# Router logits built from unnormalized tiles inside the output projection, shift and token factor applied by rows, and four picked steps in layer 0

## The reference, cut to what matters

```python
def rms_norm(x, g):
    y = x * lax.rsqrt(jnp.mean(x * x, axis=-1, keepdims=True) + NORM_EPS)
    return y * g
def modulate(h, shift, scale):
    return h * (1 + scale) + shift
...
x = x + gt1 * branch_merge(zx, o_attn_x, lp)          # ends in merged @ w_out: the "out" units
hx2 = modulate(rms_norm(x, g_norm2[l]), sh2, sc2)     # norm2
...
s = jax.nn.sigmoid(t @ w_router)                      # t: the rows of hx2 (and hc2)
sel = s + b_router                                    # best group of four, then top 2 in it
for e in range(N_EXPERTS):
    y = (jax.nn.silu(t @ w_gate[e]) * (t @ w_up[e])) @ w_down[e]
    out = out + combine[:, e:e + 1] * y
```

## Time and profile before

| | |
|---|---|
| median of 3 runs | 1436.21 us (1433.32 to 1440.65) |
| profiled execution, its own time | 1435.62 us |
| its span, first to last instruction | 1433.8 us |
| instructions | 19845 |
| busy: PE, DVE, ACT, POOL | 1242.4 us (87%), 630.7 us (44%), 365.8 us (26%), 117.0 us (8%) |
| DMA | 381.52 MB, mean 266 GB/s |
| mean granted clock | 0.949 |

### The profile page before, as it was taken

One profiled execution on the slowest core, in us unless ns is written; L12 is line 12 of the kernel. 1 busy time (PEld: TensorE's weight loads), 2 busy tenths in 40 slices (PEclk: granted clock), 3 DMA queues, 4 the chain that ended last, 5 costly groups with the idle time before them and its releaser, 6 DMA issues.

```text
span 1433.8 us, 19845 instructions
## 1 busy us (share of the span) xinstructions
PE 1242.4 (87%) x8092; PEld 783.1 (55%) x8092; DVE 630.7 (44%) x1124; ACT 365.8 (26%) x589; POOL 117.0 (8%) x107
## 2 busy tenths in 40 slices
PE   3699897899999884999998984887999977998986
PEld 1577576787787431333343334776789832443443
DVE  2627448685546350221131116485886661221222
ACT  2631125334242410100100014532544430000000
POOL 0000000000003020000000002003960200000000
PEclk9899999999999997999999997999999988999998
DMA  9747994222223549698899984785334469999996
GB/s 380 279 190 312 365 394 164 88 91 87 88 88 120 226 185 334 225 395 309 346 334 396 408 347 178 286 324 205 118 123 172 169 273 369 398 388 399 400 418 273
DMA packets 59486, 381.52 MB, mean 266 GB/s; under 512 B 8800, under 2 KB 11300, under 8 KB 19908
## 3 DMA queue, kind: packets, MB, share of 16 engines
q1 hardware_dynamic: 45584, 345.00, 61.4%
q10 hardware_dynamic: 10292, 20.44, 4.5%
q0 software_dynamic: 3520, 14.81, 2.8%
HBM read 362.66 MB, written 44.83 MB: 284 GB/s over the span
## 4 chain that ended last, share of the span: by engine, by line
PE 44%; issue 26%; DMA 13%; DVE 8%; ACT 4%; POOL 3%; SPq 1%; ACTq 0%; POOLq 0%; DVEq 0%
PE bank L1928 9%; PE bank L1929 8%; PE bank L1930 8%; DMA wexp<-in_expert 7%; PE bank L2318 3%; PE bank L2303 3%; PE bank L1895 3%; DMA stage<-in_in 2%; POOL m_lo L697 2%; DMA xT<-in_xT 1%; PE bank L1938 1%; DVE wlo L1187 1%; DMA raw<-in_mod 1%; PE bank L1998 1%; PE bank L2336 1%
## 5 line engine op out<-in xcount | busy, mean ns | idle before, releaser
L2303 PE MATMUL bank<-wexp,xg 128*64 128x512 f32 (+1 forms) x1504 | 265.4, 596 | 8.9 <-DMA wexp<-in_expert 6.3
L1928 PE MATMUL bank<-h_hi,whi 128*128 128x512 f32 (+1 forms) x640 | 226.6, 354 | 24.1 <-DVE wlo L1187 13.9
L1929 PE MATMUL bank<-h_lo,whi 128*128 128x512 f32 (+1 forms) x640 | 221.2, 346 | 0.0
L1930 PE MATMUL bank<-h_hi,wlo 128*128 128x512 f32 (+1 forms) x640 | 220.8, 345 | 0.0
L2303 PEld LDWEIGHTS bank<-wexp,xg 128*64 128x64 f32 (+1 forms) x1504 | 77.8, 125 | 160.9 <-issue 145.4
L2318 PE MATMUL bank<-wexp,act_a 128*32 128x256 f32 (+1 forms) x1072 | 147.6, 493 | 20.0 <-DMA wexp<-in_expert 13.8
L1187 DVE TENSOR_TENSOR wlo<-stage,whi 128x2048 fp32r<-128x2048 f32 x56 | 134.3, 2405 | 68.6 <-ACT whi L733 67.0
L1928 PEld LDWEIGHTS bank<-h_hi,whi 128*128 128x128 f32 x640 | 125.2, 196 | 48.7 <-DVE wlo L1187 18.9
L1187 DVE TENSOR_TENSOR act_a<-act_s,bank 128x256 f32<-128x256 f32 (+1 forms) x47 | 17.1, 364 | 287.1 <-ACT act_s L733 287.1
L733 ACT ACTIVATE whi<-stage 128x2048 fp32r<-128x2048 f32 x56 | 106.9, 1911 | 102.9 <-DMA stage<-in_in 61.3
L1929 PEld LDWEIGHTS bank<-h_lo,whi 128*128 128x128 f32 x640 | 125.3, 196 | 13.6 <-issue 0.5
(11 more groups left out here) (322 smaller groups left out, 1603.8 us busy)
## 6 DMA issues: line engine op xcount, KB each, us to landing
wexp<-in_expert SPq DMA_DIRECT2D x192, 1024.0 KB, 15.7
stage<-in_in SPq DMA_DIRECT2D x40, 1024.0 KB, 8.0
raw<-in_mod SPq DMA_DIRECT2D x18, 1024.0 KB, 8.0
stage<-in_mod SPq DMA_DIRECT2D x16, 1024.0 KB, 5.0
x_rows<-in_c_zero SPq DMA_DIRECT2D x32, 512.0 KB, 11.3
y_rows<-in_c_zero SPq DMA_DIRECT2D x20, 512.0 KB, 12.6
spare<-in_mod SPq DMA_DIRECT2D x8, 1024.0 KB, 14.4
stage<-in_out SPq DMA_DIRECT2D x8, 1024.0 KB, 4.8
```

The costliest lines, as they stand in the source:

```text
L1928: MM(o, w[0], x_[0], start=start, stop=False)
L1929: MM(o, w[0], x_[1], start=False, stop=False)
L1930: return MM(o, w[1], x_[0], start=False, stop=stop)
L2303: ins = MM(bank[0][g * w:(g + 1) * w, :], x_[:, 2 * j + k, :], wexp[:, z, j, c], start=(first_ == 0), stop=(last_ == 0))
```

## The change

The token factor r no longer goes into the tiles ahead of the router.

- ACT makes xa = xT * a (no r, no b) tile by tile within the out units. PE multiplies wr (padded with zeros to 32 columns) with xa in four strips of a bank: tiles 0 to 3 behind out unit 2 (with the product of b and wr, shift_logits), tiles 4 to 7 behind the last unit. The strips are added by a matmul with fold.
- The token factor is made for 128 tokens by NT instead of 128 copies (small, square_sums with two columns). DVE multiplies the logits with it and adds the logits of the shift.
- The rows are transposed from xa, and ACT applies r while it copies them to trow. The shift is added by rows: POOL writes it to DRAM (shift_rows, 128x8 elements of 4 bytes in turn) and loads it back to all partitions (shift_b, 512 KB each; two in layer 0, one in layer 1), counted in x_back2. POOL adds it to row tiles 2, 3 and 0 in layer 0 (0 in layer 1), two 128x512 halves each, and DVE to row tile 1. PE's pick matmuls and POOL's scatters wait for all of it, DVE's match in layer 0 for POOL's first two row tiles.
- PICKED goes from (2, 2) to (4, 2): steps 2 and 3 of layer 0 get their rows by pick matmuls behind gate(0) and gate(1), in banks 4 and 5. The first row load from x_rows is that of step 4 there.
- The first three row loads of each layer are issued by SP, ahead of the first piece of the expert ranked 10 in layer 0 and ahead of that of the one ranked 6 in layer 1 (ROWS_AHEAD), where SP waits for all scatters; ACT issued them before. The filter loads move from step 1 to step 3, and the steps of the filters' work on PE and DVE with them.

```diff
-PICKED = (2, 2)
+PICKED = (4, 2)
+ROWS_AHEAD = (10, 6)
...
@@ SP, expert loads @@
                 for r, j in plan.issue(plan.loads[LEADERS[l]:], 4, EC):
+                    if (r, j) == (ROWS_AHEAD[l], 0):
+                        sp.wait_ge(sem("all", "scattered"), sum(2 * (span(i) // P) for i in range(l + 1)) * 16)
+                        for i in range(XR - 1):
+                            row, w = plan.steps[PICKED[l] + i][3:]
+                            load(l, f"xload{i}", xpick[0:w, i, :], x_rows[l][row:row + w, :])
...
@@ POOL @@
+                for s in range(seqs(l)):
+                    pool.dma_start(shift_rows[s, :].rearrange("(k p) -> p k", p=P), modT[:, 48 + s:64:2], allow_slow_non_contiguous=True).then_inc(sem("all", "shift_out"), 16)
                 for t in range(KT):
                     pool.wait_ge(S("m_hi"), t + 1)
...
                 load("all", "x_back2", wr[:, :, :], A["router"])
+                pool.wait_ge(sem("all", "shift_out"), sum(16 * seqs(i) for i in range(l + 1)))
+                for s in range(seqs(l)):
+                    load("all", "x_back2", shift_b[s][:, :], shift_rows[s:s + 1, :].to_broadcast([P, D]))
...
+                pool.wait_ge(sem("all", "x_back2"), back2(l))
+                for t in [row_tile(l, b)[0] for b in range(NT)]:
+                    if t == 1:
+                        continue
+                    for c in range(2):
+                        b = [row_tile(l, b) for b in range(2 * NT)].index((t, c))
+                        pool.wait_ge(S("row_a"), b + 1)
+                        h = slice(c * 512, (c + 1) * 512)
+                        ins = nc.gpsimd.tensor_tensor(trow[:, t, h], trow[:, t, h], shift_b[t // 2][:, h], ADD)
+                    ins.then_inc(S("hm"), 1)
+                pool.wait_ge(S("hm"), 2 * KT + NT - 1)
+                pool.wait_ge(S("h2"), seqs(l) * KT + 1)
                 pool.wait_ge(S("rowid_ok"), 1)
-                pool.wait_ge(S("row_a"), 2 * (T // P) - 2)
-                pool.wait_ge(S("row_d"), 2)
...
@@ ACT, out_tile(k), twice in each out unit @@
+                    if k < KT - 1:
                         fn(sq[:, k % 2, 0:T], xT[:, k, 0:T], ACT.Square).then_inc(S("sq_ok"), 1)
+                    for s in range(NS):
+                        fn(xa[:, k, c], xT[:, k, c], ACT.Copy, scale=amp[:, 1, k, s:s + 1]).then_inc(S("h2"), 1)
...
@@ ACT, norm2 @@
-                fn(rs[:, 0:T], rs[:, 0:T], ACT.Sqrt).then_inc(S("root"), 1)
+                fn(lgT[:, 0:T], bank[7][:, 0:T], ACT.Copy).then_inc(S("lgT"), 1)
+                fn(small[:, 0:NT], small[:, 0:NT], ACT.Sqrt).then_inc(S("root"), 1)
                 nc.scalar.preload_act_table(ACT.Sigmoid)
-                        fn(h2T[:, k, c], hn[:, k % 2, c], ACT.Identity, scale=amp[:, 1, k, s:s + 1],
-                           bias=modT[:, 48 + 2 * k + s:49 + 2 * k + s]).then_inc(S("h2"), 1)
-                fn(rt[:, 0, 0:NT * NE], bank[7][:, 0:NT * NE], ACT.Sigmoid).then_inc(S("affin"), 1)
-                for b in range(2 * NT - 2):
+                for b in range(2):
                     rows_out_(b)
+                fn(rt[:, 0, 0:NT * NE], rt[:, 0, 0:NT * NE], ACT.Sigmoid).then_inc(S("affin"), 1)
+                for b in range(2, 2 * NT):
+                    rows_out_(b)
...
@@ DVE, norm2 @@
-                inverse_rms("n2", T, bank[2])
-                    tt(hn[:, k % 2, 0:T], xT[:, k, 0:T], rs[:, 0:T], MUL).then_inc(S("hn"), 1)
+                tt(sq[:, 1, 0:T], xT[:, KT - 1, 0:T], xT[:, KT - 1, 0:T], MUL).then_inc(S("sq_sum"), 1)
+                tt(sq_part[:, 0:T], sq_part[:, 0:T], sq[:, 0, 0:T], ADD).then_inc(S("sq_sum"), 1)
+                ts(small[:, 0:NT], bank[2][:, 0:2 * NT:2], 1.0 / D, EPS, MUL, ADD).then_inc(S("mean_sq"), 1)
+                V.reciprocal(small[:, 0:NT], small[:, 0:NT]).then_inc(S("hn"), 1)
+                v.then(tt(rt[:, 0, 0:W].rearrange("p (t e) -> p t e", e=NE), bank[7][:, 0:W].rearrange("p (t e) -> p t e", e=NE),
+                          small[:, 0:NT].unsqueeze(2).to_broadcast([P, NT, NE]), MUL))
+                tt(by_seq(rt[:, 0, 0:W]), by_seq(rt[:, 0, 0:W]), bias_, ADD).then_inc(S("lgT"), 1)
...
@@ DVE, behind mask_sums @@
-                for b in range(2 * NT - 2, 2 * NT):
-                    rows_out_(b)
+                for c in range(2):
+                    ins = tt(trow[:, 1, h], trow[:, 1, h], shift_b[0][:, h], ADD)
+                ins.then_inc(S("h2"), 1)
+                if NS == 2:
+                    dve.wait_ge(S("hm"), 2 * KT + NT // 2)
...
@@ PE, steps @@
-                for s in range(PICKED[l]):
+                for s in range(2):
                     step_rows(s)
                 step_columns(0)
                 for s in range(STEPS):
                     gate_up(*step(s))
+                    if s + 2 < PICKED[l]:
+                        step_rows(s + 2)
                     if s + 1 < STEPS:
                         step_columns(s + 1)
```

More of the change, by code:

```diff
@@ L524, in before_norm2, with back2 @@
             return KT if l == 0 else 0
+        def back2(l):
+            return sum(16 * (2 + seqs(i)) for i in range(l + 1))
         def span(l):
@@ L859, in _ @@
                         split(p)
+                    if kind == "out" and j == 0:
+                        nc.scalar.preload_act_table(ACT.Sqrt)
                     if kind == "out" and j >= 1:
-                        squares(2 * j - 2, 2 * j)
+                        for k in range(2 * j - 2, 2 * j):
+                            out_tile(k)
+                    if n == at["out", 3]:
+                        act.wait_ge(S("lg"), 1)
+                        fn(row_bias[0:2, :], bank[2][0:2, 64:64 + NE], ACT.Copy).then_inc(S("lgT"), 1)
                     if kind == "mod" and j % BATCH == BATCH - 1:
@@ L1728, in _ @@
                     v.sync()
-                    tt(pick[:, s, 0:NT * w], match[:, 0, 0:NT * w], match[:, 1, 0:NT * w], ADD).then_inc(S("picked"), 1)
+                    if s >= 3:
+                        dve.wait_ge(S("rows"), 2 * NT + s - 2)
+                    tt(pick[:, s % 3, 0:NT * w], match[:, 0, 0:NT * w], match[:, 1, 0:NT * w], ADD).then_inc(S("picked"), 1)
                     dve.wait_ge(S("picked"), s + 1)
@@ L2059, in _ @@
                             ins.then_inc(S("zr"), 1)
+                    if n == at["out", 2]:
+                        pe.wait_ge(sem("all", "x_back2"), back2(l))
+                        shift_logits()
+                        token_logits(0, 4)
                     if n == at["out", 3]:
-                        part_sums()
+                        spread_shift()
                     if kind == "mod" and j == BATCH - 1:
@@ L2286, in step_rows @@
                         for g in range(n):
[L2287 removed]
+                            ins = MM(picked_rows(s)[1][g * w:(g + 1) * w, 0:dn], pick[:, s % 3, t * w:(t + 1) * w], trow[:, t, g * dn:(g + 1) * dn], start=(t == 0), stop=(t == NT - 1))
                     ins.then_inc(S("rows"), 1)
```

196 lines of the change are left out of this document (114 added, 82 removed).

## The result

The changed kernel took 1422.65 us, median of 9 runs (1419.20 to 1430.60); the kernel before took 1435.78 in the same number of runs (1431.28 to 1440.65). The ratio is 0.9911, 95% interval 0.9891 to 0.9931: by the ratio 12.8 us faster (the two medians are 13.1 apart). A second group of runs gave 0.9912 (0.9887 to 0.9937), 1424.92 us. The forecast was 1418 with a range of 1407 to 1429.

The account below looks back on a forecast made before the run. Layer 0's experts were taken as bound by PE's 19.5 us wait for step 2's rows, layer 1 by loads. Gains of 3.2 (router), 15 (steps) and −0.5 (layer 1) summed to 17.7 us: 1418, range 1407 to 1429.

Parts of the forecast that it names:

- the router of layer 0: Layer 0, out units through router: first pick matmul at about 508.5 instead of 511.7, 3.2 us gained (0 to 7).
- the picked steps: Layer 0, gate(0) to columns of step 4: 62.4 us become 46.3, 15 gained after some 1 us wait.
- the rest of layer 0: Layer 0 behind step 4: everything shifts as one, since slots and PE set the pace together; 0 us.
- the rival of the full lock: POOL and DVE lock each other whole: layer 0's router gains 0, layer 1 one less; 1422 us, chance 0.12.
- signs of being wrong: Gain at layer 0's step 4 columns missing at layer 1's start, or layer 1 longer by over 4 us.
- Out units: Layer 0: logits of four tiles 3.45 us and shift products 1.1 make the last xT tile 4.6 us later.
- From the end of the last tile to that of the Sigmoid: Layer 0's router: from the last xT tile at 486.6 to the Sigmoid's end at about 494.3.
- POOL beside DVE: Layer 0's router: five POOL shift adds of 1.5 us slow DVE's chain by 3.5 us (bounds 0 and 7.5).
- Steps 0 to 4: Layer 0, gate(0) to columns of step 4: 46.3 us without wait, rows landing at + 47, 15 us gained.
- the rival that the loads of 740 to 850 take the gain back: Layer 0: earlier PE only waits longer for loads, at worst half of the 16 lost; 1427 us, chance 0.12.
- Layer 1: Router starts gate(0) 2.5 us earlier, SP's wait for scatters dries the loads some 3 us; net −0.5.
- The slower rival: Both layers' out units: broadcast shift loads land late, DVE's fifth tile waits; up to 1454 us, chance 0.06 (0.04 slower).

Follow-up runs that it names:

- the first profile: Profiled execution of the changed kernel, the slowest of its nine runs: 1430.6 us.
- the control: The changed kernel run once more with no edit: 1424.92 us, ratio 0.9912 to the kernel before; its profiled execution took 1423.8 us.

## Why the prediction was right, and where its terms were off

The forecast of 17.7 us less was right in direction, and the 12.8 measured lie in its range. There is luck in that: the router of layer 0 gave 2 to 3 us more than forecast, the picked steps 4 to 6 less, and 4 to 6 more went in the rest of layer 0, for which the forecast had 0. It was also luck that the rival of the full lock named 1422, next to the median, for it had the router of layer 0 gain nothing, and it gained over 5. Of the forecast's own signs of being wrong, the first profile showed one: from layer 0's last xT tile to the end it took 4.6 us longer than before (the bound was 4). In the control it was 0.6 shorter. Point by point:

**Out units (forecast +4.6, measured +1.6).** The step that failed is "the weight loads and 512 columns at the 0.43 us that each shows in the steady part make 0.86 a tile". Four tiles go to four strips of 32 partitions of the bank and took 1.07 us together, not 3.45; shift_logits took 0.53, not 1.1. The Trainium skill (TensorE: Matmul & The Clock Gate, Part 3: Packing small matmuls — row/col tiling) says that matmuls whose outputs start at different 32-partition strips run in the array at the same time. The trace agrees: eight passes in four strips took 1.07 us, two in one strip 1.04. Rows of before could have told: a pick pass, in one of two strips of 64, costs 0.215 us at full clock, half of the 0.43 of a pass with wr.

**From the end of the last tile to that of the Sigmoid (7.7 forecast, 7.4 measured).** Right: 482.8 to 490.2.

**POOL beside DVE (+3.5 forecast, +5.0 measured, 5.2 by the control and the run without the adds).** The step that failed is "DVE runs at a half to two thirds of its pace". In the chain a POOL add stops one DVE instruction until it ends, while reductions keep their 0.17. This is the rule that I had weighed (the Trainium skill, SBUF — State Buffer, Who interferes with whom), and the trace now agrees with it per instruction. One of 128x16 with a scalar (495.01, 1.19 us) was stopped too.

The earlier trace rows were misread. POOL's 1.9 us there are no price of POOL's instruction, for POOL waited in them for DVE; one of the same size takes 1.23 in the chain. And DVE lost only 0.38 because its instruction came when POOL's had 0.5 us left (one starts at 428.05, where POOL's, begun at 426.79, ends at 428.53). Single instructions of the kernel before, just behind that stretch:

```profile
437.51 3.38 DVE L1187 TENSOR_TENSOR wlo<-stage,whi 128x2048 fp32r<-128x2048 f32 x1
438.70 3.31 POOL L697 TENSOR_TENSOR m_lo<-merged,m_hi 128x512 fp32r<-128x512 f32 x1
...
440.82 3.34 DVE L1187 TENSOR_TENSOR wlo<-stage,whi 128x2048 fp32r<-128x2048 f32 x1
```

Undisturbed, wlo takes 2.29. The first loses 1.1 us to the m_lo ahead of it, which ends at 438.75; then POOL's m_lo takes 3.31, 2.1 more than 1.23, and ends 1.1 us behind that wlo; then the second wlo loses 1.0 to it. They take turns, each for a whole instruction. So the full lock, which I had given 0.12, is what the kernel before already showed. That its price was 5.0 and not the 7.5 of its bound is mostly the length of an add, 1.23 where I took 1.5: five adds are 6.1 us, less the 1.0 that the stopped instructions take anyway and 0.4 that reductions and gaps used between them, and 0.25 more were lost at the first add (490.34, 0.48 instead of 0.23).

The two errors, 3.0 us one way and 1.5 the other, cancel in part: the first pick matmul came 5.6 to 5.9 us earlier and gate(0) 5.1 to 5.9, forecast 3.2.

**Steps 0 to 4 (−15 forecast, −8.9 to −11.1 measured).** The costs of PE were right: 45.9 us once nothing waits (forecast 46.3). The step that failed is "I put their landing at + 47": it was + 53.4 (51.3 in the control). SP issued them when forecast (31.1 and some 8), at + 38.9, but they took 12.3 to 14.9 us, since the first landed only behind the last 1 MB piece ahead of it. Ahead of two of these pieces, and issued 5.7 us sooner, PE didn't wait for them. With the filter loads out of the way too they took 9.5 to 10.6 instead of 11.0 to 12.6. With the wait comes a cost that the sum didn't have, down(2) at the low clock, 2.4 to 2.9 us.

**The rest of layer 0 (0 forecast, +4.4 to +5.6 measured).** "Everything behind shifts as one" held for the steps, by some 14 us from step 4 on; the rival that the loads of 740 to 850 take the gain back falls, for even the lead of the later filter loads was kept to the last step. What the term had at nothing are down(2) and the combine, above.

**Layer 1.** Sigmoid 3.6 us earlier behind POOL's load (forecast 3.5), POOL's adds +1.5 (forecast +1.0), gate(0) −1.7 (forecast −2.5). The dry stretch of the loads is there, some 3 us up to SP's next piece at 1195.5; from gate(0) to the end 1.0 to 2.6 us were lost (forecast 3), of which none is resolved in the whole time.

**The slower rival** didn't occur: the shift loads landed 6.7 to 7.6 us behind their issue in both layers of the two profiles, and the fifth out tile waited for PE alone.

## What to carry to other kernels

Price a load by what stands ahead of it in its issuer's program and queue, not by when its data is ready: three loads of 0.5 MB in all cost this kernel 8 to 10 us for standing behind two pieces of an expert that nobody needed yet. When a wait of PE goes, look for the next landing due (here PE's rows, then ACT's own writes) and for the clock behind it. Work handed to POOL wasn't free here while DVE ran a chain of small instructions: each of POOL's last five adds held one of them up until it ended. Before taking a price from rows in which two engines overlap, look at single instructions: the mean of POOL's had its waiting in it.
